# A delta-rule scan with operands stacked on both halves of the array, and norms that no longer pass through rows

## What is computed

```python
def step(S, inp):
    r_t, w_t, k_t, v_t, kk_t, a_t = inp
    sa = jnp.einsum('bhvk,bhk->bhv', S, -kk_t)
    S = S * w_t[:, :, None, :] + sa[..., None] * (kk_t * a_t)[:, :, None, :] + v_t[..., None] * k_t[:, :, None, :]
    return S, jnp.einsum('bhvk,bhk->bhv', S, r_t)
```

## Time and profile before

| what | value |
|---|---|
| median of 3 runs | 2249.27 us (2247.49 to 2250.12) |
| profiled execution | 2246.76 us |
| its span | 2244.9 us |
| mean granted clock of TensorE | 0.983 |
| busy: TensorE, VectorE, ScalarE, GpSimd | 2117.5, 1121.6, 938.4, 1136.6 us |
| scan of group 1 | about 908 to 1066 us |
| its post norm, attention's preparation and attention | about 1066 to 1198 us |

### The profile page before, as it was taken

The page is one execution under the profiler, slowest core; times in us unless marked ns, Lnnn a source line. Parts: engine busy times, 40 slices in busy tenths (PEclk is TensorE's granted clock), DMA queues, the critical chain, the costliest instruction groups (busy, mean ns, idle before and its releaser), DMA issues. The chain is left out here.

```text
span 2244.9 us, 42906 instructions
## 1 busy us (share of the span) xinstructions
PE 2117.5 (94%) x17042; PEld 1972.2 (88%) x17042; DVE 1121.6 (50%) x2048; ACT 938.4 (42%) x1888; POOL 1136.6 (51%) x933
## 2 busy tenths in 40 slices
PE   5989999899999998999998999999999989899998
PEld 4878887799999987888788999999889877799998
DVE  5673345455665237433554566632664255457740
ACT  4422335445444433232463444444432355355542
POOL 5543333365666654333334656665543333567775
PEclk8999999999999999999999999999999999999999
DMA  5421122363444433112225534444321333644453
GB/s 177 147 67 58 57 85 91 126 213 113 127 126 145 147 123 94 49 48 79 91 78 184 173 113 127 126 149 139 116 76 54 91 112 97 195 152 147 146 159 123
DMA packets 158150, 264.86 MB, mean 118 GB/s; under 512 B 20096, under 2 KB 53120, under 8 KB 157952
## 3 DMA queue, kind: packets, MB, share of 16 engines
q1 hardware_dynamic: 157376, 261.08, 37.2%
q10 hardware_dynamic: 576, 1.05, 0.1%
HBM read 242.60 MB, written 19.46 MB: 117 GB/s over the span
## 5 line engine op out<-in xcount | busy, mean ns | idle before, releaser
L215 POOL TENSOR_TENSOR k_w_lo<-k_raw,k_w_hi 128x512 fp32r<-128x512 f32 x832 | 1088.3, 1320 | 1016.7 <-ACT k_w_hi L206 972.6
L206 ACT ACTIVATE k_w_hi<-k_raw 128x512 fp32r<-128x512 f32 x832 | 500.0, 617 | 383.4 <-PE k_acc L237 129.3
L235 PE MATMUL k_acc<-k_x_hi,k_w_hi 128*128 128x384 f32 (+1 forms) x1152 | 416.6, 362 | 15.0 <-PEq L70 10.0
L237 PE MATMUL k_acc<-k_x_hi,k_w_lo 128*128 128x384 f32 (+1 forms) x1152 | 379.1, 329 | 0.0
L236 PE MATMUL k_acc<-k_x_lo,k_w_hi 128*128 128x384 f32 (+1 forms) x1152 | 378.6, 329 | 0.0
L235 PEld LDWEIGHTS k_acc<-k_x_hi,k_w_hi 128*128 128x128 f32 x1152 | 219.2, 190 | 54.3 <-issue 29.9
L236 PEld LDWEIGHTS k_acc<-k_x_lo,k_w_hi 128*128 128x128 f32 x1152 | 219.4, 190 | 5.6 <-issue 1.4
L237 PEld LDWEIGHTS k_acc<-k_x_hi,k_w_lo 128*128 128x128 f32 x1152 | 218.5, 190 | 0.0
L235 PE MATMUL k_acc<-k_o_hi,k_w_hi 128*128 128x384 f32 (+1 forms) x288 | 98.0, 340 | 24.4 <-POOL k_w_lo L215 9.7
L235 PE MATMUL k_acc<-g0f_xg_hi,k_w_hi 128*128 128x384 f32 x352 | 118.7, 337 | 2.2 <-DVE g0f_a_raw L1982 2.2
L235 PE MATMUL k_acc<-g1f_xg_hi,k_w_hi 128*128 128x384 f32 x352 | 118.7, 337 | 2.2 <-DVE g1f_a_raw L1982 2.2
(11 more groups left out here) (710 smaller groups left out, 4476.6 us busy)
## 6 DMA issues: line engine op xcount, KB each, us to landing
k_raw<-w_up SPq DMA_DIRECT2D x264, 256.0 KB, 2.8
k_raw<-w_gate SPq DMA_DIRECT2D x144, 256.0 KB, 3.1
k_raw<-w_down SPq DMA_DIRECT2D x96, 256.0 KB, 3.8
k_raw<-w_rwkv SPq DMA_DIRECT2D x84, 256.0 KB, 3.0
k_raw<-w_branch SPq DMA_DIRECT2D x72, 256.0 KB, 3.5
k_raw<-w_attn SPq DMA_DIRECT2D x60, 256.0 KB, 2.9
k_raw<-w_out SPq DMA_DIRECT2D x48, 256.0 KB, 3.0
k_raw<-w_down_end SPq DMA_DIRECT2D x24, 256.0 KB, 3.4
```

Source lines behind the costliest of these rows:

```text
L206: act.activation(c.w_hi[s][:, 0:n], c.raw[s][:, 0:n], ACT.Copy).then_inc(c.hi_done, 1)
L215: pool.tensor_tensor(c.w_lo[s][:, 0:n], c.raw[s][:, 0:n], c.w_hi[s][:, 0:n].bitcast(F32), ALU.subtract).then_inc(c.lo_done, 1)
L235: pe.matmul(out, wh, xh, start=(u.begins and k == 0), stop=False)
L237: mm = pe.matmul(out, wl, xh, start=False, stop=(u.ends and k == u.kt - 1))
```

## The change

The scan: the state's tiles become [128, 8, 64]. For a head, one half of the partitions holds the state and the other half v, later sa; `xr` holds the decayed operand in one half and the masked product with k in the other. So one product of all 128 rows does what two of 64 rows did and added (`stacked`), and its output goes to one half of the array's columns. b and k lie side by side (`bk_s`), so gram and tok take both at once with 128 columns of weights (`b_and_k`). The part of the output that needs only the old state goes ahead of sa. Matmuls a chunk, the turn of v included: 144 in place of 184. VectorE writes the masks and the operands by halves, 29 operations a chunk for 21; ScalarE's copies of v, tok and sa are in two parts; GpSimd makes one scaled identity for two scaled operands, and its scaled state has twice the elements and waits for tok of both chunks.

The norms: `to_rows` and `from_rows` and their two transfers go. In prep and post norm `ones_head` gives every partition the sum of its head, in four banks; ScalarE and VectorE take the root of all four tiles, and VectorE multiplies. Attention's preparation takes the keys' root alone in that way. The queries' sums are made by eight products with 32 columns of weights on four column strips, copied, and turned by six transposes, so that a token's root is a scalar of its partition, `qf`, that the bias and the exponentials apply to scores. The queries' gains go into the keys (`kq`, and the memory keys). `N_POST` is 11. All nine squares have a tile of their own, and TensorE waits for all of them before its first product. Some tiles of the feed-forward block lie at another address.

```diff
-N_PREP, N_POST, N_ATTN_PREP = 14, 9, 8
+N_PREP, N_POST, N_ATTN_PREP = 14, 11, 8
 GATE_STORES = 3 * DT // 2
 N_KEYS = 4
+ROOM = 9488
...
-                pe.wait_ge(S["tan"], 2 + 7)
+                pe.wait_ge(S["tan"], 2 + 8)
+                pe.wait_ge(S["g_done"], 2)
                 pe.wait_ge(S["sq_done"], 1)
                 for m in range(4):
-                    mm = pe.matmul(bank[0][:, 0:T], c.to_rows[:, m, :], sq[:, m, 0:T], start=(m == 0), stop=(m == 3))
-                mm.then_inc(S["rows"], 1)
-                yield
-                yield
-                yield
-                pe.wait_ge(S["p_root"], ROOT)
-                pe.wait_ge(S["g_done"], 4)
-                products(*((b, c.from_rows[:, m, :], y[:, 0:T]) for m, b in ((0, 5), (1, 0))))
-                yield
-                pe.wait_ge(S["got"], 2)
-                products(*((b, c.from_rows[:, m, :], y[:, 0:T]) for m, b in ((2, 5), (3, 0))))
-                pe.wait_ge(S["tan"], 10)
+                    pe.matmul(bank[m][:, 0:T], c.ones_head[:, :], sq[:, m, 0:T], start=True, stop=True).then_inc(S["rows"], 1)
+                yield
+                yield
+                pe.wait_ge(S["p_root"], 1)
                 pe.wait_ge(S["dstep"], 5)
-                products(*((1 + m, c.ones_head[:, :], t3[:, m, 0:T]) for m in range(4)))
+                products(*((m, c.ones_head[:, :], t3[:, m, 0:T]) for m in range(4)))
...
+            def turn_across(out, tile):
                 for j in range(4):
-                    for h in H:
-                        mm = pe.matmul(out[h, j, :], tile[h, j, :], c.ident[h, h], start=True, stop=True)
+                    for e, h in enumerate(H):
+                        mm = pe.matmul(out[H[1 - e], j, :], tile[h, j, :], c.ident[h, h], start=True, stop=True)
                 return mm
+            def stacked(out, lhs, rhs, stop=True):
+                for j in range(4):
+                    for e, h in enumerate(H):
+                        mm = pe.matmul(out[h, j, :], lhs[:, 4 * e + j, :], rhs[:, 4 * e + j, :], start=(stop or j == 0),
+                                       stop=stop)
+                return mm
+            def b_and_k(u, e, j):
+                return bk_s[u][H[e], j, :]
...
-                        heads(bank_b[u], (b_s[u], ar_s[u]))
-                        heads(bank_c[u], (k_s[u], ar_s[u])).then_inc(S["gram"], 1)
+                        for j in range(4):
+                            for e, out in enumerate((bank_b[u], bank_c[u])):
+                                mm = pe.matmul(out[:, j, :], b_and_k(u, e, j), xr[u][H[e], 4 * e + j, :], start=True,
+                                               stop=True)
+                        mm.then_inc(S["gram"], 1)
...
-                        turn(heads8[4 + u][:, 0:4, :], b_s[u])
-                        turn(heads8[4 + u][:, 4:8, :], k_s[u]).then_inc(S["tok"], 1)
+                        for j in range(4):
+                            for e, h in enumerate(H):
+                                mm = pe.matmul(bk_out[u][e][:, j, :], b_and_k(u, e, j), ident_pc[u][h, j, :], start=True,
+                                               stop=True)
+                        mm.then_inc(S["tok"], 1)
...
-                        heads(bank_a[u][:, 0:4, :], (ar_s[u][:, :, 0:C], old), (lk[u], v_t[u])).then_inc(S["xs"], 1)
+                        stacked(bank_a[u][:, 0:4, :], xr[u][:, :, 0:C], old).then_inc(S["xs"], 1)
                         yield
                         pe.wait_ge(S["t3_read"], n + 1)
+                        stacked(bank_b[u][:, :, 0:C], old, xr[u][:, :, C:2 * C], stop=False)
                         pe.wait_ge(S["xs_read"], n + 1)
                         heads(bank_c[u][:, :, 0:C], (m2[u], sx)).then_inc(S["sa"], 1)
                         yield
                         pe.wait_ge(S["sa_read"], n + 1)
-                        heads(bank_a[u][:, 0:4, :], (bk_t[u][:, 0:4, :], sa),
-                              (bk_t[u][:, 4:8, :], v_t[u])).then_inc(S["ssum"], 1)
-                        heads(bank_b[u][:, :, 0:C], (old, ar_s[u][:, :, C:2 * C]), (v_t[u], mk[u]),
-                              (sa, mb[u])).then_inc(S["osum"], 1)
+                        stacked(bank_a[u][:, 0:4, :], bk_t[u], old).then_inc(S["ssum"], 1)
+                        for j in range(4):
+                            for e, h in enumerate(H):
+                                mm = pe.matmul(bank_b[u][h, j, 0:C], old[h, 4 * e + j, :], mb[u][h, j, :], start=False,
+                                               stop=(j == 3))
+                        mm.then_inc(S["osum"], 1)
...
-                    mm = pe.matmul(bank[4][:, 0:T], c.to_rows[:, m, :], nsq[:, m, 0:T], start=(m == 0), stop=(m == 3))
-                mm.then_inc(S["var"], 1)
-                yield
-                yield
-                yield
-                pe.wait_ge(S["n_root"], ROOT)
-                for m in range(4):
-                    pe.wait_ge(S["centred"], 4)
-                    pe.matmul(bank[m][:, 0:T], c.from_rows[:, m, :], ny[:, 0:T], start=True, stop=True).then_inc(S["spread"], 1)
-                yield
-                yield
-                yield
-                yield
+                    pe.matmul(bank[m][:, 0:T], c.ones_head[:, :], nsq[:, m, 0:T], start=True, stop=True).then_inc(S["var"], 1)
+                for _ in range(9):
+                    yield
 
             def attn_prep():
                 yield
-                for ns in (range(0, 4), range(4, 8), range(8, 9)):
-                    for n in ns:
-                        pe.wait_ge(S["a_squared"], n + 1)
-                        pe.matmul(bank[5][:, 0:T], c.to_rows[:, n, :], asq[:, n % 4, 0:T], start=(n == 0),
-                                  stop=(n == 8)).then_inc(S["a_rows"], 1)
-                    yield
-                yield
-                yield
-                pe.wait_ge(S["a_root"], ROOT)
-                pe.wait_ge(S["post"], 4)
-                for n in range(9):
-                    if n >= 5:
-                        pe.wait_ge(S["a_done"], n - 4)
-                    pe.matmul(bank[n % 5][:, 0:T], c.from_rows[:, n, :], ay[:, 0:T], start=True,
-                              stop=True).then_inc(S["a_spread"], 1)
-                    if n in (4, 8):
-                        yield
+                yield
+                yield
+                pe.wait_ge(S["a_squared"], 9)
+                pe.matmul(bank[5][:, 0:T], c.ones_head[:, :], asq[:, 4, 0:T], start=True, stop=True).then_inc(S["a_rows"], 1)
+                pe.wait_ge(S["n_root"], 1)
+                for j in range(4):
+                    rows = slice(32 * j, 32 * j + 32)
+                    pe.matmul(bank[4][rows, 0:T], c.ones_head[:, 0:P:4], asq[:, j, 0:T], start=True, stop=True)
+                for j in range(4):
+                    rows = slice(32 * j, 32 * j + 32)
+                    mm = pe.matmul(bank[0][rows, 0:T], c.ones[:, 0:32], asq[:, 5 + j, 0:T], start=True, stop=True)
+                mm.then_inc(S["q_rows"], 1)
+                yield
+                yield
+                pe.wait_ge(S["q_read"], 1)
+                for n, b in enumerate((4, 0)):
+                    for p, it in enumerate(items):
+                        mm = pe.transpose(bank[b][0:it.nq, p * P:(p + 1) * P], q_rows[:, n, it.q0:it.q0 + it.nq], c.ident[:, :])
+                mm.then_inc(S["q_turned"], 1)
...
+                        for e, h in enumerate(H):
+                            ins = act.activation(state_in(n, u)[h, 4 * e:4 * e + 4, :], bank_c[u][h, :, 0:C], ACT.Copy)
+                        ins.then_inc(S["sa_read"], 1)
...
+            def operands_bk(us_):
                 for n, u, early in us_:
                     tok = slice(n * C, (n + 1) * C)
                     dve.wait_ge(S["decays"], n + 1)
                     if not early:
+                        dve.wait_ge(S["tok"], n - 1)
+                    for e, h in enumerate(H):
+                        dve.tensor_tensor(bk_s[u][h, :, H[e]], ar[h, X_B, tok], en[u][h, :, :], ALU.mult)
+                        dve.tensor_tensor(bk_s[u][h, :, H[1 - e]], ar[h, X_K, tok], en[u][h, :, :], ALU.mult)
+            def operands(us_):
+                for n, u, early in us_:
+                    tok = slice(n * C, (n + 1) * C)
+                    if not early:
                         dve.wait_ge(S["osum"], n - 1)
                         dve.wait_ge(S["s0p"], n - 1)
-                    dve.scalar_tensor_tensor(ar_s[u][:, :, 0:C], ar[:, X_KK, tok], -1.0, ep[u][:, :, 0:C], ALU.mult, ALU.mult)
-                    dve.tensor_tensor(ar_s[u][:, :, C:2 * C], ar[:, X_R, tok], ep[u][:, :, 1:C + 1], ALU.mult)
-                    dve.tensor_tensor(b_s[u][:, :, :], ar[:, X_B, tok], en[u][:, :, :], ALU.mult)
-                    dve.tensor_copy(pc[u][:, :, :], ep[u][:, :, C:C + 1])
-                    dve.tensor_tensor(k_s[u][:, :, :], ar[:, X_K, tok], en[u][:, :, :], ALU.mult).then_inc(S["operands"], 1)
```

(84 more changed lines are left out.)

205 lines of the change are left out of this document (122 added, 83 removed).

## The result

The changed kernel takes 2269.5 us in the median of 4 runs (2265.16 to 2272.95), the kernel before 2249.69 beside it: ratio 1.0085, 95% interval 1.007 to 1.010. It is slower by some 20 us. Forecast were 2217 and a gain. The profiled execution has a span of 2271.1 us for 2244.9; at 2272.95 us it is the slowest of the four, so the profile shows a loss of 26 us where the medians have 20.

The account below looks back on a forecast made before the run. TensorE, busy 94% of the span, was taken as the bound, most fully in the scan. Terms -35 + 10 + 4 - 14 + 4 - 1 = -32 gave 2214.8 us profiled, 2217 as a median, range 2203 to 2229.

Parts of the forecast that it names:

- TensorE's work: Fewer matmuls: -35 us in the scan over 17 chunks, -32 in post norm and attention's preparation; prep loses four spreading products.
- rival E: Scan: stacked products bound by their weight loads, 58 ns an instruction, +20 us, 2237 in all; chance 0.08.
- rival D: New shapes do not run together at all: +53 us in the scan, +12 in the strips, 2282; chance 0.06.
- Scan, VectorE: Half masks make TensorE wait longer for the second chunk's transpose: +10 us over 8 pairs, bounds 0 to +24.
- +1.5 a group: Scan's start: the slow stretch at clock 0.50 moves from inside a wait to there, costing 1.5 us.
- Prep norm: Prep to the scan's start: spreading products go, VectorE's chain grows, the wait moves; +4 us over three groups (-8 to +12).
- a first gram about 1 us later: Scan's start: VectorE's longer chain to the first operands delays the first gram by about 1 us.
- Post norm: Post norm and attention's preparation: -32 us of work, +18 of waits and clock, sum -14 (-32 to 0).
- the wait of 8: Post norm: TensorE waits 8 to 9 us, taken as 8, for all nine squares before its first product.
- +2 a group: Post norm and attention's preparation: the clock falls behind the wait for the squares, costing 2 us.
- +0.2 a half: Attention: bias as four operations of 256 elements for two of 512, +0.2 us in each of 20 halves.
- Rival C: VectorE falls further behind: 3 us a pair (+14) and Newton steps locked out by GpSimd (+6), 2237; chance 0.13.

Follow-up runs that it names:

- e1: Kernel before with the changed scan alone, every norm and the rows as before: 2244.88 us, ratio 0.999.
- e5: Changed kernel with VectorE's transpose moved ahead of four half masks, no work added or taken: 2239.85 us, ratio 0.9965.
- e6: Changed kernel with three thrown-away products on TensorE while it waits for the second chunk's transpose: 2256.17 us, ratio 1.0038.
- e9: Changed scan with all norms of the kernel before, the early transpose, and the first chunk's operands completed before the second's: 2229.67 us, ratio 0.9911.
- e8: Changed kernel with prep's three Newton steps put together and the first chunk's operands completed before the second's: 2257.84 us, ratio 1.0049.
- e7: Changed kernel with thrown-away products during the transpose wait, 12 more ahead of the wait for prep and 6 ahead of the first gram: 2254.36 us, ratio 1.0027.
- e3: Changed kernel with the prep norm of the kernel before, through rows: 2252.74 us, ratio 1.0016.

## Why the prediction was wrong

- **TensorE's work** was right: in e1 the scan saved 35.0 us of it, the forecast's 35; behind the scan some 34 went for 32, in prep 6.8 for 7.8. The stacked products ran two at a time, and rival E (bound by weight loads) and rival D fell. Rival E priced them at 58 ns an instruction; the trace has 16 in 0.69 us with equal row groups, as many as 64*64 products in 0.68. The rule of the Trainium skill, "TensorE: Matmul & The Clock Gate", Part 3, is that a weight load overlaps running matmuls only where the row group differs; this trace does not agree.
- **Scan, VectorE** is the step that failed first: +10 forecast for the waits, 16.5 measured, and 20.5 by a clock for which the scan had no term: 37 in all. Two errors. A half mask was taken at 0.33 and took 0.44, so the waits for the transpose in a group were 6.3 to 6.9 and not 4 to 5. And I charged the fall of the clock behind the long known waits, but not behind these. Of the 41.0 us that TensorE is busy at the lower clock in the scan, 25 lie behind these waits (9 in group 0, 9 in group 1, twice 3 in group 2), worth an estimated 12.6; e5 and e6 take most of them away and gain 27 and 11 us. The rest lies at the scan's start, where the prediction had put +1.5 a group.
- **Prep norm:** the wait at the scan's start was foreseen (8.2 and 4.6 us; I wrote about 10), but it was priced at +4 and cost +15. The failed step is "a first gram about 1 us later": the prediction's own terms for VectorE's chain add up to +4.2 us a group (3.6 + 2 - 0.5 + 2.8 - 3.7), and nothing is said of what should hide the other 3. The stretch grew by 4.7 to 5.4 a group. The scan's operands cost 3.2 of that (e1), where the term was +2.8; more than half of it is the order, b and k of both chunks ahead of the first queries (e9). A Newton step also was caught in VectorE's queue behind an add that waits for TensorE (e8). The +1.5 for the clock was too much for the changed scan (under 1 in e7).
- **Post norm:** the wait of 8 came as 5.2 + 2.9, its first part at another instruction, L235, whose accumulator VectorE's chain had not read. Work was right. The term that was mis-sized most is the clock, +2 a group: it cost an estimated 18.2 us in all; in group 1 the clock falls four times in this stretch. Waits grew by 24.6, where the other terms come to some 16. In group 1 the first scores wait 2.0, the softmax's products 5.7 for 2.0, the memory scores 2.7 for 1.3; "+0.2 a half" for the bias does not hold these. How much of the softmax's wait is the bias and how much the late, slow start of the scores, no run tells apart.
- In sum, forecast -32, measured +26 of span: the scan misses 22, prep 11, post norm and attention 23, the rest 2. With the moved 4 us put back where they were saved, the scan misses 26 and what is behind it 19. In the median it is 2269.5 for 2217. Rival C (VectorE falls further behind) was the nearest in its mechanism, but it too left out the clock behind these waits. Rival D's 2282 is nearer by number alone: what it stands on, new shapes that do not run together, did not happen.

## What to carry to other kernels

A matmul saved is worth its time only while the engine that feeds the next one keeps up: work out when each operand is made on the helping engine, per chunk, before counting TensorE's gain. A wait of two or three microseconds on TensorE can cost more than itself, if TensorE comes back at the lower clock. Here that followed the same wait in some groups and runs and not in others. So look in the windows for a granted clock under 1.00 right behind a wait, in more than one trace, and order the helper's stream so that what TensorE needs next is made first. And check that a slow stretch lies where TensorE sets the pace before spending anything on it.

## What was not expected of the hardware

- VectorE operations on half of the partitions are dearer when they alternate halves. The second of these three stays on the first one's half and comes 0.34 behind it, the third changes halves and comes 0.42 behind:

```profile
918.26 0.42 DVE L1345 TENSOR_TENSOR g1m_room<-g1m_ar,g1m_room 64x256 f32<-64x256 f32 x1 [0.42 <-ACT g1m_room L1049]
918.60 0.41 DVE L1346 TENSOR_TENSOR g1m_room<-g1m_ar,g1m_room 64x256 f32<-64x256 f32 x1
919.02 0.42 DVE L1345 TENSOR_TENSOR g1m_room<-g1m_ar,g1m_room 64x256 f32<-64x256 f32 x1
```

  The masks alternate at every step and come 0.44 apart; on all partitions it was 0.33. That the crossing is the cause was not tested by itself.
- The length of a wait does not tell by itself whether the clock falls. The wait of 2.88 or 2.89 us for the transpose of the second pair stands in groups 0 and 1 of the changed kernel, e3 and e8. The clock was at the lower level behind it in four of the six, and stayed at 1.00 in e3's group 1 and e8's group 0. The wait of 2.19 ahead of group 2's last chunk was followed by the lower clock in the changed kernel and e6, and not in e1, e3, e7 and e8. Behind the waits for the transpose of under 2 us it stayed at 1.00 in all of these traces. What decides in between, no run shows.
- Eight products with 32 columns of weights, on four column strips, 384 columns each, took 1.51 us for 8 instructions at a granted clock of 0.50 and 1.01 for the next 8 at 0.83, where the same number with all columns takes 2.74; strips do run together.
